# Matrix memory in a two-block kernel: gate rows spread over the partitions by DMA instead of by TensorE products

## Chip, cores and metric

One core of a Trainium2 chip. The metric is the device time of one execution, in microseconds (us).

## What is computed

Two transformer-like blocks over 512 tokens of width 1024, in float32. The first has sparse attention and a linear recurrence. The second has a matrix memory (mLSTM), a differential attention, a merge of the two and a mixture of 32 small experts. The change touches only the matrix memory, with 4 heads of 128 dimensions. Cut to what matters, the reference is:

```python
bcum = jnp.cumsum(ft, axis=-1)
dmat = jnp.where(causal, bcum[..., :, None] - bcum[..., None, :] + it[..., None, :], -jnp.inf)
m_t = jnp.maximum(m_inter, jnp.max(dmat, axis=-1))
s = jnp.einsum('bhtd,bhsd->bhts', qt, kt) * jnp.exp(dmat - m_t[..., None])
num = jnp.einsum('bhts,bhsd->bhtd', s, vt) + ...
den = jnp.maximum(jnp.abs(den), jnp.exp(-m_t))
h = num / den[..., None]
```

The kernel does not go by chunks of 64 with a carried state. It forms the whole causal 512 x 512 matrix of weights of a head, `exp(row[t] + column[s])` times the qk scores, in four strips of 128 keys.

## The kernel before

All engines run one long hand-ordered program. Every wait is written out, and a `Banks` object deals out the eight PSUM banks: `B.take(lo, hi, ...)` gives the banks from lo to hi - 1 in turn, and the wait on `u.free` is for the reader of that bank's last use. Each engine works through its functions in the order of `tensor_program`, `scalar_program`, `vector_program`, `pool_program` and `sync_program` (L3390 to L3544).

In block 2, projections write q, k, v and the gates. `dve_gates2` (L2079) computes the running sums of the gates with the heads in 4 partitions. Its results are `CI`, the column part, and `RA[j]` (4 partitions x 512), the row part for key strip j, valid from column 128 j. `CI` is turned into `COLI` (128 keys on the partitions). At the end of `pe_block2` (L1993) q and k of the differential attention are transposed into eight banks, which `act_block2` evicts (L2042).

Then comes the matrix memory: `pe_mlstm` (L2152), `act_mlstm` (L2180) and `dve_mlstm` (L2212), over heads h = 0 to 3 and key strips j = 0 to 3, with n = 512 - 128 j query columns. For each strip:

- PE: a row product (L2159) spreads row h of `RA[j]` over 128 partitions, into bank 0 or 1; it multiplies by a 4 x 128 selector made of one column of the identity.
- PE: the qk product (L2164), into bank 2, 3 or 4.
- DVE: adds the causal mask to the first 128 columns of the row, in PSUM (L2219).
- ACT: exponential with the column part as bias, PSUM to `WB[x]` in SBUF (L2192).
- DVE: multiplies qk scores, weights and a scale into `SB[h % 2]` (L2225).

After the strips PE computes a tile of the differential attention's values for the head (`vd`, `pe_tokens2`, L1938: eight chunks of 128 x 128 by 512 columns, two passes each), and then the last head's `mv` products (L2176), weights times values, with the row sum in column 129. ACT and DVE turn these into the normalised output (L2202 to L2236). The stage ends with the `mv` products of head 3. `pe_diff` (L2306) begins behind it.

On SP's queue, `sp_block2` (L1790 on) loads block 2's input weights in slots: `cm1` and `va` at L1800 and L1801, `om` at L1803, `vd` at L1805. `sp_merge2` (L2428) issues the two branch weights (`pm` L2431, `pd` L2432) when the last `va` product is done, then the gate weights in four parts (L2440, `part`), the late modulation weights and the output weight. `sp_experts` (L3103) starts with the merge's last output. `GBC` holds a row tile for the residual scaling later and is free during the matrix memory; `W[1]` holds the `va` weights until the last `va` product, and then `pd`.

Of the kernel before, what the change touches and what calls it, by code (L numbers as in the profile page):

```python
# [157 lines left out]
def build(nc, A, out, CD, COFF, CSMALL):  # L158
# [3 lines left out]
    def sig(*names, step=1):  # L162
        made = [Count(nc.alloc_semaphore(n), step) for n in names]
        counts.extend(made)
        return made if len(made) > 1 else made[0]
# [88 lines left out]
    xnd = nc.dram_tensor("scr_xn", [S, D], F32).ap()  # L254
    xd = nc.dram_tensor("scr_x", [S, D], F32).ap()
    modd = nc.dram_tensor("scr_mod", [2, D], F32).ap()

    o = 0

# [88 lines left out]
    CB = [omf[:, 0:1030], WIQ[:, 3072:4102]]  # L348
    HM, HD = QDR, KDR
    kdr = KDR.rearrange("p i d -> p (i d)")  # L350
    WB = [kdr[:, 1280:1792], PB2[0]]
    SB = [kdr[:, 0:1280], omf[:, 0:1280]]
    SB2 = [CV[0][:, 0:512], CV[1][:, 0:512]]
    HMT, HDT = QM, KM
# [66 lines left out]
    last_in = [sig(f"last_gates{e}_in", f"last_ups{e}_in", step=16) for e in (NP - 2, NP - 1)]  # L421
    exp_in = sig(*[f"expert{i}_in" for i in range(NE)], step=16)
    mod_out, mod_back = sig("mod_out", "mod_back", step=16)
    early_ada_in = sig("early_ada0_in", "early_ada1_in", step=16)
    part_in = sig("ada_half0_in", "ada_half1_in", step=16)
    b1_in = sig("b1_in", step=16)
# [1361 lines left out]
    def sp_block2(sp, ws):  # L1788
        ws.wait_ge(*B.use("pa", 7).full)
        sp.dma_start(WIQ.rearrange("p (c n) -> p c n", c=8), wsrc(w2in, 2048, 520)).then_inc(*ring[0].up("qd"))  # L1790
        ws.wait_ge(*B.use("wo", 2, 1).full)
        ws.wait_ge(*out7_pool.at("S", 4))
        sp.dma_start(wv(2, 8, 512), wsrc(w2in, 2568, 512)).then_inc(*ring[2].up("kd"))
        ws.wait_ge(*B.use("wo", 4, 1).full)
        sp.dma_start(wv(3, 8, 512), wsrc(w2in, 0, 512)).then_inc(*ring[3].up("cm0"))
        for i in range(NT - 1):
            sp_spill(sp, ws, i)
        sp_spill(sp, ws, NT - 1)
        ws.wait_ge(*B.use("kd", 4).full)
        sp.dma_start(wv(2, 8, 512), wsrc(w2in, 512, 512)).then_inc(*ring[2].up("cm1"))  # L1800
        sp.dma_start(wv(1, 8, 512), wsrc(w2in, 1024, 512)).then_inc(*ring[1].up("va"))  # L1801
        ws.wait_ge(*B.use("cm0", 4).full)
        sp.dma_start(wv(3, 8, 512), wsrc(w2in, 1536, 512)).then_inc(*ring[3].up("om"))  # L1803
        ws.wait_ge(*B.use("cm1", 4).full)
        sp.dma_start(wv(2, 8, 512), wsrc(w2in, 3080, 512)).then_inc(*ring[2].up("vd"))  # L1805

    def sp_spill(sp, ws, i):

# [343 lines left out]
    def pe_mlstm(pe, wp):  # L2152
        for h in range(5):
            if h < 4:
                for j in range(4):
                    n = 512 - 128 * j
                    u = B.take(0, 2, "row", h, j)
                    wp.wait_ge(*u.free)
                    pe.matmul(u.ap[:, 0:n], fv(ident[0:4, h:h + 1], [[0, 128]]), RA[j][0:4, 128 * j:512],  # L2159
                              start=True, stop=True).then_inc(*u.filled)  # L2160
                    u = B.take(2, 5, "mqk", h, j)
                    wp.wait_ge(*u.free)
                    wp.wait_ge(*qk_act.at(7))
                    pe.matmul(u.ap[:, 0:n], KM[:, h, tile(j)], QM[:, h, 128 * j:512], start=True, stop=True).then_inc(*u.filled)  # L2164
                pe_tokens2(pe, wp, "vd", 2, h, 7, 8)
            if h:
                for q in range(2):
                    u = B.take(5, 7, "mv", h - 1, q)
                    wp.wait_ge(*u.free)
                    wait_halves(wp, "va")  # L2170
                    wp.wait_ge(*set_dve.at("va"))
                    for i in (2 * q, 2 * q + 1):
                        for j in range(i + 1):
                            wp.wait_ge(*B.use("mqk", h - 1, j).out)
                            o0 = offs[j] + (i - j) * 128
                            t = pe.matmul(u.ap[:, 129 * (i % 2):129 * (i % 2) + 129], SB[(h - 1) % 2][:, o0:o0 + 128],  # L2176
                                          VA[:, j, h - 1, :], start=j == 0, stop=j == i)
                    t.then_inc(*u.filled)

    def act_mlstm(act, wa):  # L2180
        for h in range(5):
            if h < 4:
                for j in range(4):
                    n, x = 512 - 128 * j, (4 * h + j) % 2
                    u = B.use("row", h, j)
                    if h == 0 and j < 2:
                        wa.wait_ge(*B.use("dT", 1, 3).full)
                        wa.wait_ge(*B.use("ci").out)
                    else:
                        wa.wait_ge(*B.use("mqk", h - (j < 2), (j - 2) % 4).out)  # L2190
                    wa.wait_ge(*mw_dve.at("mask", h, j))
                    act.activation(WB[x][:, 0:n], u.ap[:, 0:n], ACT.Exp, bias=COLI[:, j, h:h + 1]).then_inc(*u.read)  # L2192
                u = B.use("vd", h)
                wa.wait_ge(*u.full)
                act.activation(VD[:, h, :], u.ap, ACT.Copy).then_inc(*u.read)
            if h:
                for q in range(2):
                    u = B.use("mv", h - 1, q)
                    if h > 1:
                        wa.wait_ge(*B.use("mv", h - 2, q).out)  # L2200
                    wa.wait_ge(*u.full)
                    act.activation(DEN[:, 2 * q:2 * q + 2], fv(u.ap[:, 128:129], [[129, 2]]), ACT.Abs).then_inc(*den_act.up(h - 1, q))  # L2202
                for i in range(NT):
                    wa.wait_ge(*B.use("mv", h - 1, i // 2).out)
                    if i > 1:
                        wa.wait_ge(*hm_act.at(h - 1, i - 2))
                    elif h > 1:
                        wa.wait_ge(*hm_act.at(h - 2, i + 2))
                    act.activation(kdr[:, 1792 + 128 * (i % 2):1920 + 128 * (i % 2)], HM[:, i, tile(h - 1)], ACT.Square,
                                   accum_out=HS3[:, 4 * i + h - 1:4 * i + h]).then_inc(*hm_act.up(h - 1, i))  # L2210

    def dve_mlstm(dve, wd):  # L2212
        for h in range(5):
            if h < 4:
                for j in range(4):
                    n, x = 512 - 128 * j, (4 * h + j) % 2
                    u = B.use("row", h, j)
                    wd.wait_ge(*u.full)
                    dve.tensor_tensor(u.ap[:, 0:128], u.ap[:, 0:128], k("masksT"), ALU.add).then_inc(*mw_dve.up("mask", h, j))  # L2219
                    v = B.use("mqk", h, j)  # L2220
                    if h > 1:
                        wd.wait_ge(*B.use("mv", h - 2, 1).full)
                    wd.wait_ge(*u.out)
                    wd.wait_ge(*v.full)
                    dve.scalar_tensor_tensor(out=SB[h % 2][:, offs[j]:offs[j] + n], in0=v.ap[:, 0:n], scalar=msc,  # L2225
                                             in1=WB[x][:, 0:n], op0=ALU.mult, op1=ALU.mult).then_inc(*v.read)
            if h:
                for q in range(2):
                    u = B.use("mv", h - 1, q)
                    d = DEN[:, 2 * q:2 * q + 2]  # L2230
                    wd.wait_ge(*den_act.at(h - 1, q))
                    dve.tensor_tensor(d, d, fv(COLM[:, 2 * q, h - 1:h], [[4, 2]]), ALU.max).then_inc(*den_dve.up("max", h - 1, q))
                    wd.wait_ge(*den_dve.at("max", h - 1, q))
                    dve.reciprocal(d, d).then_inc(*den_dve.up("r", h - 1, q))
                    wd.wait_ge(*den_dve.at("r", h - 1, q))
                    dve.tensor_tensor(HM[:, 2 * q:2 * q + 2, tile(h - 1)], fv(u.ap[:, 0:1], [[129, 2], [1, 128]]),  # L2236
                                      fv(d, [[1, 2], [0, 128]]), ALU.mult).then_inc(*u.read)
# [189 lines left out]

    def sp_merge2(sp, ws):  # L2428
        ws.wait_ge(*B.use("va", 4).full)
        ws.wait_ge(*qk_dve.at(7, 3))  # L2430
        sp.dma_start(wv(0, 4, 1024), wsrc(A["w_br_m_2"][0], 0, 1024)).then_inc(*ring[0].up("pm"))  # L2431
        sp.dma_start(wv(1, 4, 1024), wsrc(A["w_br_d_2"][0], 0, 1024)).then_inc(*ring[1].up("pd"))  # L2432
        for part in range(4):
            if part < 2:
                ws.wait_ge(*B.use(("vd", "om")[part], 3).full)
# [2 lines left out]
            w = W[2 + part % 2].rearrange("p (g c n) -> p g c n", g=2, c=8)  # L2438
            for n, g0 in enumerate((3592, 4616)):
                sp.dma_start(w[:, n], wsrc(w2in, g0 + 256 * part, 256)).then_inc(*ring[2 + part % 2].up("g2", part))  # L2440
            if part == 2:
                ws.wait_ge(*B.use("hmT", 3).full)
                ws.wait_ge(*B.use("hdT", 3).full)
# [1152 lines left out]
```

## Time and profile before

| | us |
|---|---|
| runs | 1286.52, 1273.55, 1278.89 |
| median of the three | 1278.89 |
| the profiled execution's own time | 1281.12 |
| span in its trace | 1279.3 |
| PE busy | 1204.9 (94%) |
| DVE busy | 593.0 (46%) |
| POOL busy | 312.6 (24%) |
| ACT busy | 307.8 (24%) |

Times in the trace count from the start of the span. PE stands for TensorE's products and PEld for its weight loads, which overlap them; DVE is VectorE, ACT ScalarE, POOL GpSimd, and SPq the queue in which SyncE issues transfers. The matrix memory's stage runs from about 651 to 718 us. A float32 product appears as two instructions (x2).

### The profile page before, as it was taken

How to read it: one execution, taken by the hardware profiler on the slowest of the kernel's cores; microseconds unless marked ns; L12 is line 12 of the kernel's file. 1: busy time of each engine (PE TensorE's matmuls, PEld its weight loads, DVE VectorE, ACT ScalarE, POOL GpSimd, SP SyncE). 2: the span in 40 equal slices, each digit the busy share in tenths (PEclk: the TensorE clock that was granted, in tenths of full speed). 3: DMA queues.
4: the chain of work that ended last, by engine and by line, in shares of the span. 5: the costliest groups of instructions: out<-in, count | busy, mean ns of one | idle time of the engine just before them, and what ended most of it. 6: DMA issues, size and time to landing. Idle time of an engine off the chain costs nothing.

```text
span 1279.3 us, 13740 instructions
## 1 busy us (share of the span) xinstructions
PE 1204.9 (94%) x5120; PEld 707.7 (55%) x5120; DVE 593.0 (46%) x1441; ACT 307.8 (24%) x715; POOL 312.6 (24%) x241
## 2 busy tenths in 40 slices
PE   7999999999999999999999999999899999988884
PEld 3555444445578444788855558577464674433342
DVE  2357375376632243259932476574442543222221
ACT  4302644343322001331122354100011321111110
POOL 7300012355571531264300300231100121211100
PEclk9999999999999999999989999999899999998998
DMA  9849105124224014105130202622449599999995
GB/s 317 183 149 273 66 1 132 66 91 140 70 96 169 28 67 142 56 6 192 67 131 1 67 1 66 203 90 75 99 176 350 195 333 389 409 399 406 413 401 203
DMA packets 95530, 214.97 MB, mean 168 GB/s; under 512 B 20190, under 2 KB 54382, under 8 KB 83640
## 3 DMA queue, kind: packets, MB, share of 16 engines
q1 hardware_dynamic: 81940, 192.62, 41.7%
q0 software_dynamic: 10320, 18.80, 6.0%
q10 hardware_dynamic: 3196, 2.61, 0.6%
q8 instruction: 43, 0.70, 0.2%
q14 instruction: 31, 0.25, 0.1%
HBM read 207.30 MB, written 14.75 MB: 174 GB/s over the span
## 4 chain that ended last, share of the span: by engine, by line
PE 70%; DVE 12%; SPq 8%; DMA 3%; ACT 3%; issue 2%; POOL 0%; POOLq 0%; DVEq 0%; ACTq 0%
PE PS L2533 8%; SPq L3084 7%; PE PS L1046 6%; PE PS L1496 4%; PE PS L1704 4%; PE PS L2712 4%; PE PS L2596 3%; PE PS L3216 3%; PE PS L673 3%; PE PS L1938 2%; PE PS L532 2%; DMA AN<-in_w_up 2%; PE PS L1950 2%; PE PS L1892 2%; PE PS L1524 2%; PE PS L1516 2%
## 5 line engine op out<-in xcount | busy, mean ns | idle before, releaser
L1046 PE MATMUL PS<-HT,W 128*128 128x512 f32 x256 | 125.4, 613 | 1.4 <-ACT AN L1210 1.4
L1310 POOL TENSOR_SCALAR AN<-AN,SM 128x128 f32<-128x128 f32 (+3 forms) x64 | 72.6, 1143 | 220.5 <-DVE SM L1418 220.5
L1344 DVE SCALAR_TENSOR_TENSOR AN<-AN,COLA 128x256 f32<-128x256 f32 x168 | 96.7, 576 | 6.1 <-DMA AN<-in_w_ada 1.0
L3216 PE MATMUL PS<-AN,HT 128*64 128x512 f32 x192 | 61.5, 632 | 9.8 <-DMA X<-in_w_up 6.0
L2511 POOL TENSOR_TENSOR AN<-W 128x512 f32<-128x512 f32 x8 | 10.2, 1271 | 235.3 <-DMA W<-in_w_in 99.7
L3301 DVE TENSOR_TENSOR HT<-HT,PS 128x256 f32<-128x256 f32 x16 | 6.7, 421 | 130.3 <-ACT HT L3276 130.3
L2596 PE MATMUL PS<-AN,W 128*128 128x512 f32 x128 | 58.7, 616 | 8.1 <-DVE AN L2652 8.1
L1046 PEld LDWEIGHTS PS<-HT,W 128*128 128x128 f32 x256 | 44.7, 194 | 39.0 <-issue 36.1
L2712 PE MATMUL PS<-W,AN 128*128 128x512 f32 x128 | 57.1, 595 | 0.0
L1291 ACT ACTIVATE AN<-PS,SM 128x128 f32<-128x128 f32 (+3 forms) x64 | 33.7, 526 | 94.7 <-DVE SM L1397 94.4
L3276 ACT ACTIVATE HT<-PS 128x256 f32<-128x256 f32 x16 | 6.1, 384 | 183.9 <-PE PS L3216 155.8
L3216 PEld LDWEIGHTS PS<-AN,HT 128*64 128x64 f32 x192 | 20.7, 145 | 47.8 <-issue 47.8
L2596 PEld LDWEIGHTS PS<-AN,W 128*128 128x128 f32 x128 | 25.0, 198 | 39.5 <-issue 28.8
L673 PE MATMUL PS<-W,HT 128*128 128x280 f32 (+1 forms) x128 | 43.6, 498 | 0.0
L3216 PE MATMUL PS<-W,HT 128*64 128x512 f32 x160 | 37.0, 616 | 5.7 <-DMA W<-in_w_up 5.7
L3237 PE MATMUL PS<-W,HT 128*64 128x512 f32 x160 | 36.5, 597 | 6.1 <-DVE HT L3306 6.1
L1385 DVE COPY AN<-PS 128x128 f32<-128x128 f32 (+3 forms) x32 | 15.6, 487 | 56.4 <-PE PS L1141 56.4
L2712 PEld LDWEIGHTS PS<-W,AN 128*128 128x128 f32 x128 | 23.5, 190 | 25.8 <-issue 25.8
L3158 POOL DMA_INDIRECT out<-GBC,SM x8 | 12.6, 1572 | 96.6 <-DVE GBC L3316 96.6
L3158 POOL DMA_INDIRECT out<-AN,SM x8 | 12.6, 1580 | 95.0 <-DVE AN L3316 69.1
L1141 PEld LDWEIGHTS PS<-K,AN 128*128 128x128 f32 x160 | 19.1, 142 | 26.6 <-issue 25.7
L673 PEld LDWEIGHTS PS<-W,HT 128*128 128x128 f32 x128 | 24.0, 190 | 17.5 <-issue 14.8
(566 smaller groups left out, 2474.2 us busy)
## 6 DMA issues: line engine op xcount, KB each, us to landing
W<-in_w_in SPq DMA_DIRECT2D x13, 2048.0 KB, 8.6
W<-in_w_down SPq DMA_DIRECT2D x20, 1024.0 KB, 27.6
AN<-in_w_gate SPq DMA_DIRECT2D x17, 1024.0 KB, 24.6
AN<-in_w_up SPq DMA_DIRECT2D x17, 1024.0 KB, 25.7
AN<-in_w_ada SPq DMA_DIRECT2D x16, 1024.0 KB, 6.0
AN<-in_w_down SPq DMA_DIRECT2D x12, 1024.0 KB, 26.6
W<-in_w_in SPq DMA_DIRECT2D x11, 1024.0 KB, 8.4
W<-in_w_gate SPq DMA_DIRECT2D x10, 1024.0 KB, 22.8
```

The costliest lines, as they stand in the source:

```text
L673: t = pe.matmul(u.ap[:, 0:nw], hT[:, c, tile(i)], wv(slot, 8, nw)[:, c, :], start=c == 0, stop=c == 7)
L1046: t = pe.matmul(u.ap, w[:, c, tile(m)], hT[:, c, :], start=c == 0, stop=c == 7)
L1310: pool.tensor_scalar(PU[u % 5][:, 0:n], PU[u % 5][:, 0:n], RSUM[:, u:u + 1], None, ALU.mult).then_inc(*sc_pool.up(u))
L1344: dve.scalar_tensor_tensor(out=a, in0=wt[:, c, :], scalar=ca["c2"][:, c:c + 1], in1=a, op0=ALU.mult, op1=ALU.add).then_inc(*ada_dve.up(p, c))
L1496: m = pe.matmul(u.ap[:, 256 * h:256 * h + 256], s[:, c, tile(2 * pair + h)], t[:, c, :], start=c == 0, stop=c == 3)
L1704: m = pe.matmul(u.ap, t[:, c, tile(j)], s[:, c, :], start=c == 0, stop=c == 3)
L2533: m = pe.matmul(u.ap[:, 0:256], s[:, c, :], t[:, c, :], start=c == 0, stop=c == 3)
L2596: t = pe.matmul(u.ap, wv(n, 4, 1024)[:, c, tile(m)], (HMT, HDT)[n][:, c, :], start=c == 0, stop=c == 3)
L2712: t = pe.matmul(u.ap, MT2[:, c, i, :], wv(2 + n, 8, 512)[:, c, :], start=c == 0, stop=c == 7)
L3084: sp.dma_start(WE[m % NE][:, 2048 * n:2048 * n + 2048], src).then_inc(*exp_in[m % NE].up(m))
L3216: t = pe.matmul(u.ap[r, :].rearrange("p (n f) -> p n f", n=2), XGT[e % 2][:, c, r], w_gu(3 * e + half)[:, c], start=c == 0, stop=c == 7)
L3237: t = pe.matmul(u.ap[r, :], AT[e % 2][:, c, r], w_dn(m, half)[:, c, n * 512:(n + 1) * 512], start=c == 0, stop=c == 1)
```

## The change

The row products leave TensorE. `RA[0]` to `RA[3]` are written to a scratch tensor `rowd` [4, 1280] in DRAM, the valid columns of the four strips side by side (offsets `offs` = 0, 512, 896, 1152). For each head one transfer then reads row h of it with a partition step of 0 and fills a [128, 1280] tile `WB[h]` in SBUF: head 0 in `GBC`, heads 1 to 3 in `W[1]`. The mask is added and the exponential taken in place there. The four masks of a head now stand together (`dve_row_masks`), those of head h+1 behind the score products of head h. The qk products get the banks 0 to 4. Transfers: the four writes and row 0's load go into `sp_block2` ahead of the load of `om`, with a wait for the writes; the loads of rows 1 to 3 go ahead of `pm`; `pd`, whose slot they use, moves behind the gate weights' part 0 and a wait for the last score product.

```diff
+    rowd = nc.dram_tensor("scr_row", [4, 1280], F32).ap()
-    WB = [kdr[:, 1280:1792], PB2[0]]
+    WB = [GBC[:, 0:1280]] + [W[1][:, 1280 * n:1280 * n + 1280] for n in range(3)]
...
         sp.dma_start(wv(1, 8, 512), wsrc(w2in, 1024, 512)).then_inc(*ring[1].up("va"))
+        ws.wait_ge(*if_dve.at("ra", 3))
+        for j in range(4):
+            n = 512 - 128 * j
+            sp.dma_start(rowd[:, offs[j]:offs[j] + n], RA[j][0:4, 128 * j:512]).then_inc(*gate_row_out.up())
+        ws.wait_ge(*sg_act.at("ga", 0))
+        ws.wait_ge(*gate_row_out.at())
+        sp_row(sp, ws, 0)
         ws.wait_ge(*B.use("cm0", 4).full)
...
+    def sp_row(sp, ws, h):
+        row = rowd[h:h + 1, :]
+        sp.dma_start(WB[h], bass.AP(tensor=row.tensor, offset=row.offset, ap=[[0, 128], [1, 1280]])).then_inc(*gate_row_in[h].up())
... pe_mlstm
-                    u = B.take(0, 2, "row", h, j)
-                    wp.wait_ge(*u.free)
-                    pe.matmul(u.ap[:, 0:n], fv(ident[0:4, h:h + 1], [[0, 128]]), RA[j][0:4, 128 * j:512],
-                              start=True, stop=True).then_inc(*u.filled)
-                    u = B.take(2, 5, "mqk", h, j)
+                    u = B.take(0, 5, "mqk", h, j)
... act_mlstm
-                    act.activation(WB[x][:, 0:n], u.ap[:, 0:n], ACT.Exp, bias=COLI[:, j, h:h + 1]).then_inc(*u.read)
+                    act.activation(v, v, ACT.Exp, bias=COLI[:, j, h:h + 1]).then_inc(*mw_act.up(h, j))
... dve_mlstm
+    def dve_row_masks(dve, wd, h):
+        wd.wait_ge(*gate_row_in[h].at())
+        for j in range(4):
+            d = WB[h][:, offs[j]:offs[j] + 128]
+            dve.tensor_tensor(d, d, k("masksT"), ALU.add).then_inc(*mw_dve.up("mask", h, j))
...
+        dve_row_masks(dve, wd, 0)
+        wd.wait_ge(*B.use("dT", 1, 3).full)
...
-                    dve.tensor_tensor(u.ap[:, 0:128], u.ap[:, 0:128], k("masksT"), ALU.add).then_inc(*mw_dve.up("mask", h, j))
...
+                if h < 3:
+                    dve_row_masks(dve, wd, h + 1)
... sp_merge2
         ws.wait_ge(*B.use("va", 4).full)
+        for h in range(1, 4):
+            sp_row(sp, ws, h)
         ws.wait_ge(*qk_dve.at(7, 3))
-        sp.dma_start(wv(1, 4, 1024), wsrc(A["w_br_d_2"][0], 0, 1024)).then_inc(*ring[1].up("pd"))
...
+            if part == 0:
+                ws.wait_ge(*B.use("mqk", 3, 3).out)
+                sp.dma_start(wv(1, 4, 1024), wsrc(A["w_br_d_2"][0], 0, 1024)).then_inc(*ring[1].up("pd"))
```

## Rows read from the trace of the kernel before

**Rows 1.** The page: each engine's busy time, its share of the span, instructions.

```profile
PE 1204.9 (94%) x5120; PEld 707.7 (55%) x5120; DVE 593.0 (46%) x1441; ACT 307.8 (24%) x715; POOL 312.6 (24%) x241
```

**Rows 2.** Busy time by stretch, us (x instructions), then PEclk, DMA share, GB/s.

```profile
core 0: us, PE busy (x) PEld busy (x) DVE busy (x) ACT busy (x) POOL busy (x), PEclk, DMA share, GB/s
...
691.20:705.50 14.30, 14.30 (x51) 7.08 (x49) 4.09 (x14) 3.90 (x15) 0.00 (x0) 1.00 0.00 0
...
720.00:775.00 55.00, 52.98 (x213) 27.36 (x212) 41.14 (x155) 27.94 (x99) 10.13 (x8) 1.00 0.03 7
```

**Rows 3.** The chain that ended last, in order of time: start, length, what.

```profile
706.31 6.87 PE PS L1938 x16
713.18 2.25 PE PS L2176 x20
716.53 1.84 PE PS L2176 x14
...
781.68 20.74 PE PS L2533 x96
...
1120.43 1.88 SPq L3084
```

**Rows 4.** Timeline, heads 0 and 2: start, length, engine, instruction, [idle before].

```profile
651.15 1.12 PE L2159 MATMUL PS<-AN,K 4*128 4x512 f32 x2 [0.57 <-ACT AN L2042]
...
659.36 9.45 PE L1938 MATMUL PS<-W,HT 128*128 128x512 f32 x16
...
685.40 1.12 PE L2159 MATMUL PS<-AN,K 4*128 4x512 f32 x2
...
686.45 1.13 PE L2164 MATMUL PS<-AN 128*128 128x512 f32 x2
...
687.50 0.91 PE L2159 MATMUL PS<-AN,K 4*128 4x384 f32 x2
...
688.34 0.91 PE L2164 MATMUL PS<-AN 128*128 128x384 f32 x2
...
691.17 7.03 PE L1938 MATMUL PS<-W,HT 128*128 128x512 f32 x16
```

**Rows 5.** Timeline, ACT: the eight evictions ahead of the stage.

```profile
647.57 4.03 ACT L2042 ACTIVATE AN<-PS 128x512 f32<-128x512 f32 x8 [4.94 <-PE PS L1993]
```

**Rows 6.** PE alone by stretch: busy us (x), PEclk, DMA share, GB/s.

```profile
651.15:653.00 1.85, 1.85 (x4) 1.00 1.03 423
653.00:659.36 6.36, 6.36 (x14) 0.58 0.88 355
659.36:664.10 4.74, 4.74 (x7) 0.50 0.00 0
...
668.73:674.56 5.83, 5.83 (x18) 0.99 0.00 0
674.56:677.60 3.04, 3.04 (x5) 0.50 0.02 5
677.60:683.07 5.47, 5.47 (x13) 0.98 0.00 0
```

**Rows 7.** Groups of 646 to 722 us by form: busy us, mean ns | idle before.

```profile
L2219 DVE TENSOR_TENSOR PS<-PS,K 128x128 f32<-128x128 f32 x16 | 4.7, 294 | 15.5 <-PE PS L2159 15.4
...
L2192 ACT ACTIVATE AN<-PS,SM 128x512 f32<-128x512 f32 x4 | 2.7, 677 | 0.9 <-DVE PS L2219 0.8
...
L2192 ACT ACT_TABLE_LOAD x1 | 1.3, 1283 | 1.1 <-DVE PS L2219 1.1
```

**Rows 8.** Timelines of DVE and of SP's queue ahead of the stage.

```profile
572.48 0.27 DVE L2095 TENSOR_TENSOR AN<-AN 4x128 f32<-4x128 f32 x1
...
573.87 0.58 SPq L1801 DMA_DIRECT2D W<-in_w_in  x1
597.62 0.37 SPq L1803 DMA_DIRECT2D W<-in_w_in  x1
...
646.39 0.37 SPq L2431 DMA_DIRECT2D W<-in_w_br_m  x1
```

**Rows 9.** DMA issues of the whole run: queue, x, KB each, median us to landing.

```profile
AN<-scr_line POOLq DMA_DIRECT2D x1, 1024.0 KB, 17.2
...
scr_line<-AN POOLq DMA_DIRECT2D x1, 64.0 KB, 5.1
```

More of the change, by code:

```diff
@@ L423, in build @@
     mod_out, mod_back = sig("mod_out", "mod_back", step=16)
+    gate_row_out = sig("gate_rows_out", step=16)
+    gate_row_in = sig(*[f"gate_row{h}_in" for h in range(4)], step=16)
     early_ada_in = sig("early_ada0_in", "early_ada1_in", step=16)
@@ L2183, in act_mlstm @@
                 for j in range(4):
[L2184 to L2187, printed above, removed]
+                    v = WB[h][:, offs[j]:offs[j] + 512 - 128 * j]
+                    if h == 0 and j == 0:
                         wa.wait_ge(*B.use("ci").out)
-                    else:
-                        wa.wait_ge(*B.use("mqk", h - (j < 2), (j - 2) % 4).out)
                     wa.wait_ge(*mw_dve.at("mask", h, j))
-                    act.activation(WB[x][:, 0:n], u.ap[:, 0:n], ACT.Exp, bias=COLI[:, j, h:h + 1]).then_inc(*u.read)
+                    act.activation(v, v, ACT.Exp, bias=COLI[:, j, h:h + 1]).then_inc(*mw_act.up(h, j))
                 u = B.use("vd", h)
@@ L2215, in dve_mlstm @@
                 for j in range(4):
-                    n, x = 512 - 128 * j, (4 * h + j) % 2
-                    u = B.use("row", h, j)
-                    wd.wait_ge(*u.full)
-                    dve.tensor_tensor(u.ap[:, 0:128], u.ap[:, 0:128], k("masksT"), ALU.add).then_inc(*mw_dve.up("mask", h, j))
+                    n = 512 - 128 * j
                     v = B.use("mqk", h, j)
@@ L2222, in dve_mlstm @@
                         wd.wait_ge(*B.use("mv", h - 2, 1).full)
-                    wd.wait_ge(*u.out)
+                    wd.wait_ge(*mw_act.at(h, j))
                     wd.wait_ge(*v.full)
                     dve.scalar_tensor_tensor(out=SB[h % 2][:, offs[j]:offs[j] + n], in0=v.ap[:, 0:n], scalar=msc,
-                                             in1=WB[x][:, 0:n], op0=ALU.mult, op1=ALU.mult).then_inc(*v.read)
+                                             in1=WB[h][:, offs[j]:offs[j] + n], op0=ALU.mult, op1=ALU.mult).then_inc(*v.read)
+                if h < 3:
+                    dve_row_masks(dve, wd, h + 1)
             if h:
```

## The prediction

> **What bounds the kernel now.** I read the page first. TensorE (PE) is busy for 94% of the span [rows 1], so the question is whether the stream around the change is PE's own. The table by stretch comes next: from 691.2 to 705.5 us, one head of the matrix memory, PE is busy all the time while DVE and ACT are busy for 4.1 and 3.9 of 14.3 us [rows 2]. The chain of waits says the same. It runs through the value products of line 1938 and the products of line 2176, head after head, up to 716.53 + 1.84 = 718.4 us. After that it goes on through the differential attention, the merge and the routing, in pieces of PE, DVE and ACT, and enters SP's queue of expert loads at 1120 us, where transfers hold it [rows 3]. None of the pieces from 718 to 1120 us is a transfer or tied to a fixed time; each begins when the stage before has given it something, and the first expert load waits for the merge. So what the memory's stage gives up should move the rest of the program as a block.
>
> Inside a head PE's order is: four times a row product and a qk product, then 16 value products (eight chunks, two passes each). The row products stand in that stream in full view. In head 2, where nothing waits and the clock is full, the block from 685.40 to the first value product at 691.17 is 5.77 us long. Its starts split it: 1.05 us for a row product of 512 columns, 0.84 for 384, so 0.21 for each 128, which gives 0.63 and 0.42 for the other two. Row products take 2.94 us, and 2.83 are left for the qk products [rows 4]. In head 0 the same block takes 659.36 - 651.15 = 8.21 us: a later row product waits for its bank, and for that DVE's mask, ACT's exponential and DVE's product have to run.
>
> **The change part by part.**
>
> *Row products removed.* Heads 1, 2 and 3 are each shorter by about 2.9 us at full clock (head 1's block is 5.83 us long [rows 6], head 3's like head 2's): 8.8 us.
>
> *Head 0.* The qk products now take the banks 0 to 4 in turn, so in head 0 they wait for no DVE or ACT work of this stage. The first needs bank 0, which the old first row product got at 651.15. Bank 1 is free when the last transpose is evicted, at 647.57 + 4.03 = 651.60 [rows 5], before the second product wants it at 652.20. The block takes 2.83 us in place of 8.21: 5.4 us gained.
>
> *The clock.* The granted clock was 1.00 up to 653, 0.58 on average to 659.36, 0.50 to 664.10 and again from 674.56 to 677.60 [rows 6]; in the later heads it was 1.00 [rows 2]. Both falls come in or just behind a block of row and qk products, the first with waits in it, and both times the value products that follow, one behind the other, brought the clock back to its full level of 2.4 GHz. Head 0's value products took 668.73 - 659.36 = 9.37 us and head 1's 683.07 - 674.56 = 8.51 [rows 6], against 6.87 in head 3 [rows 3]. Without the thin stretches I expect both at 6.87: 2.5 + 1.6 = 4.1 us gained. This is the least certain term, because PE never stopped for more than 0.57 us before the first fall [rows 4].
>
> The Trainium skill ("TensorE: Matmul & The Clock Gate", Part 1) says that the array's clock falls after it has been idle. By that sentence alone row products that keep PE busy are not to blame, the low clock stays, and the 4.1 us drop out of the sum. The same page's section on a second failure mode reports falls from many short stops between groups, which keeps them in. No row here decides between the two.
>
> *Mask and exponential.* The 16 mask additions took 0.29 us each in PSUM, an exponential at most 0.68 us, its table load 1.28 [rows 7]. They stay, with operands in SBUF. A 128-column addition in SBUF took 0.27 us on DVE [rows 8]; bounds for the 16 are half and twice that, 2 to 9 us, in a stage in which DVE is free for over two thirds. The masks of head h+1 stand behind the products of head h; the exponentials of head 0 start at 651.60 + 1.28 = 652.9 and end by 655.6. PE comes back to bank 0 with head 1's second product at about 662. Nothing is added to the sum. If this cover were gone, one head's chain (1.28 + 2.7 + 0.7 us) would be the price, once.
>
> *Row writes and row 0, in SP's queue.* The rows are ready at 572.48 + 0.27. Four writes from 4 partitions follow the loads of line 1801 (573.87), then SP waits for them and issues row 0's spread load, all before the load of `om` at 597.62 [rows 8]. Two 2 MB loads are ahead in the queue. The nearest row for the writes is 64 KB to DRAM from 8 partitions, landed after 5.1 us [rows 9]; bounds are 5 us and, behind 4.2 MB at 423 GB/s [rows 6], 15 us. The spread load is 128 partitions x 5 KB = 0.66 MB, all from the same 5 KB; the trace has no such load of that size. The nearest is the bias line's read, 1 MB into 128 partitions from overlapping addresses, landed after 17.2 us beside other transfers, 61 GB/s [rows 9]. The other end is the rate of the weights at 651 us, 423 GB/s. So row 0 is in between about 583 and 600 us, and it is needed at 651. `om`, needed at 718, may leave some 5 us late. Cost zero.
>
> *Rows 1 to 3* leave at 646.39, ahead of the two branch weights [rows 8]. At 61 GB/s they land at 657, 668 and 679, at 423 GB/s before 656 even with five microseconds for the landing. In the new stream head 1's exponentials follow head 0's value copy at about 661, head 2's come at 673, head 3's at 685. I take the slow end: slack 4 to 6 us. The first branch weight is in by 685 and needed behind the gate products that end at 802 [rows 3]. Cost zero.
>
> *The second branch weight* moves behind the first gate weights, to about 695 us. DMA is nearly idle there (0.03 from 720 to 775 us [rows 2]) and its product comes after 802. Cost zero.
>
> *Sum.* 5.4 + 2.5 for head 0, 2.9 + 1.6 for head 1, 2.9 + 2.9 for heads 2 and 3: 18.2 us. The stage built anew says the same: 651.15 + 2.83 + 6.87 = 660.9; head 1 at 670.6, head 0's values 2.3 us to 672.9, head 2 at 682.6, values to 684.9, head 3 at 694.6, and 5.4 us of last values as now: 700.0 against 718.4. The profiled run took 1281.12 us, so 1262.9. The median of the runs shown, 1278.89, is 2.2 us lower, which puts the changed kernel at 1260.7; I say 1261.
>
> **The rivals.**
>
> *The clock stays low* (0.20). If the fall at 653.9 has its cause before the stage, it stays in place: 10.2 us at 0.50 under a dense stream cost 5.1, and the second fall's 3.0 us cost 1.5. The gain is then 13.1 without the second fall, 11.6 with it: 1266 to 1267 us. For it: PE had been thin for under 3 us when the clock fell. Against: the blocks of heads 2 and 3, which wait for nothing, are followed by full clock. By the idle rule of the Trainium skill named above it would come out so.
>
> *The gain is given back later* (0.12). The differential stage starts on ACT's chain, the experts end on bandwidth. If the merge or the expert loads keep their present time, all but a few microseconds are lost, some 1277 us. Against: the chain shows no transfer and no fixed time between the stage and the experts [rows 3].
>
> *A spread load that is too slow* (0.06), the other side. 128 reads of the same 5 KB might crawl. They hold up the stage when row 1 lands after 660, row 2 after 673 or row 3 after 685, that is under 1.97 MB / 38.6 us = 51 GB/s. The whole gain is gone when row 3 lands at 703 (35 GB/s); at 28 GB/s it lands at 716 and the kernel ends at 1279 + 13 = 1292. Against it stand the 61 GB/s of the bias line.
>
> **How the numbers follow.** The forecast has 0.62: 1261 us. The three runs shown lie 13 us apart, so a median may miss the sum by 5 us; its own range is 1255 (the lowest run less 18.2) to 1266. To leave no more than 2 in 10 outside, the range reaches through the clock case, seen from the highest run: 1286.5 - 14 = 1272. I give 1254 to 1272. What a measurement can tell from no change is about 1%, 12.8 us. Of the forecast 0.57 lie beyond it, of the clock case half, 0.10, and 0.02 of the late losses, which may be partial: faster 0.69. Slower is the slow load but for 0.01: 0.05. The rest, 0.26, is the same.
>
> **What would show it.** Right: head 0's block of qk products 2.8 to 3.0 us long; the value products of all heads 6.9 us, with the granted clock at 1.00 from 651 on; the first differential product 49 us after the first product of head 0, where it was 67; rows 1 to 3 landed within 33 us; merge and experts as long as now. Wrong: 0.50 early in the stage (first rival); DVE idle on a DMA before the masks (third); a later stage longer by what this one gave up (second).

## The result and the profile after

| us | before | after |
|---|---|---|
| median | 1279.13 (4 runs, 1273.55 to 1286.52) | 1259.83 (4 runs, 1258.83 to 1263.15) |
| profiled execution | 1281.12 | 1263.15 |
| its span | 1279.3 | 1261.3 |
| first product of head 0 to first differential product | 67.13 | 45.94 |

The ratio is 0.9841, with an interval of 0.9805 to 0.9877: 1.6% faster, clear of no change. Six further runs of the changed kernel gave 1259.62 and 0.9849 (0.9814 to 0.9884). The prediction was 1261.0 us, and the stage was to end 49 us after its start.

The page's first part (busy us, share of the span, instructions) stands against [rows 1]: PE has 32 instructions and 18.7 us of work less (and PEld 32 weight loads), and DVE, ACT and POOL have what they had.

```profile
PE 1186.2 (94%) x5088; PEld 702.6 (56%) x5088; DVE 592.2 (47%) x1441; ACT 306.7 (24%) x715; POOL 312.4 (25%) x241
```

The timeline of PE in the changed kernel (start, length, instruction, idle before) answers to [rows 4]. Line 2175 is now the qk product, 1953 the value product, 2187 `mv`, 2330 the first product of the differential attention.

```profile
651.63 2.42 PE L2175 MATMUL PS<-AN 128*128 128x512 f32 x8 [0.57 <-ACT AN L2057]
653.89 7.03 PE L1953 MATMUL PS<-W,HT 128*128 128x512 f32 x16
660.76 2.32 PE L2175 MATMUL PS<-AN 128*128 128x512 f32 x8
662.91 7.03 PE L1953 MATMUL PS<-W,HT 128*128 128x512 f32 x16
...
697.57 0.49 PE L2330 MATMUL PS<-AN 64*128 64x128 f32 x4
```

Head 0's qk block is 653.89 - 651.63 = 2.26 us long, head 1's 2.15, and the value products of both take 6.9. PE by stretch (length, busy us, granted clock, DMA share, GB/s), against [rows 6], has the clock at 1.00 in every stretch; the first and one of the later ones:

```profile
651.60:660.90 9.30, 9.27 (x25) 1.00 0.79 316
...
681.20:692.40 11.20, 11.20 (x46) 1.00 0.00 0
```

What the change put on SP's queue and its time from issue to landing (queue, x, KB each, median us), against [rows 8, 9]:

```profile
574.99 4.29 SPq L1808 DMA_DIRECT2D scr_row<-AN  x4
587.82 0.35 SPq L1820 DMA_DIRECT2D GBC<-scr_row  x1
...
646.87 1.29 SPq L1820 DMA_DIRECT2D W<-scr_row  x3
```

```profile
W<-scr_row SPq DMA_DIRECT2D x3, 640.0 KB, 5.6
...
GBC<-scr_row SPq DMA_DIRECT2D x1, 640.0 KB, 4.0
```

The four writes, issued from 574.99 us behind two loads of 2 MB, are done when row 0's load leaves at 587.82. Row 0 is in SBUF at 592 us, 60 us before it is needed. Rows 1 to 3 leave at 646.9 and are in by about 655. The masks and the exponentials by form (x | busy us, mean ns | idle before) wait for no transfer; they cost about what they cost in PSUM [rows 7]:

```profile
L2223 DVE TENSOR_TENSOR W<-W,K 128x128 f32<-128x128 f32 x12 | 2.7, 282 | 0.0
...
L2199 ACT ACTIVATE W<-W,SM 128x512 f32<-128x512 f32 x3 | 2.1, 708 | 0.0
```

**Where the gain went.** The stage is 21.2 us shorter, the span 18.0. The distance between the same instruction in the two traces tells where 3.2 us went. The stage starts 0.48 us later in the profile after (651.63 against 651.15), less than the same kernel's start moves from run to run (see the experiments). The first differential product stands 20.7 us earlier, the first gate product (line 2533 before, 2551 after) 774.38 - 754.84 = 19.5, and so does the whole merge up to the routing. There the chain of waits of before and of after (start, length, what) parts again:

```profile
1026.91 3.58 PE PS L2758 x20
...
1033.30 2.43 PE PS L2758 x20
```

```profile
1007.26 4.43 PE PS L2776 x20
...
1015.21 2.43 PE PS L2776 x20
```

1026.91 - 1007.26 = 19.65, 1033.30 - 1015.21 = 18.09. Between the two the clock is at 0.50 in both kernels, but it comes back later in the changed one. PE by stretch, before and after:

```profile
1025.00:1029.00 4.00, 3.48 (x17) 0.50 1.02 423
1029.00:1033.00 4.00, 4.00 (x43) 0.95 0.86 288
```

```profile
1006.00:1010.00 4.00, 3.48 (x17) 0.50 1.01 407
1010.00:1015.00 5.00, 5.00 (x44) 0.69 0.75 260
```

From there on the distance stays at 18.1 us as long as PE sets the pace. Where the expert loads do, behind 1120 us of the kernel before, the distance between the same loads swings between 15 and 20 us (1200.24 - 1180.52 = 19.7, 1231.03 - 1214.81 = 16.2), and it is back at 18.0 in the end. So the end moved with the rest, but the loads between do not keep one distance. Why the clock came back later in the routing is not shown. The loss of 1.2 us in the differential stage is the subject of the fourth experiment.

### The profile page after: what moved, and what is told of

It reads as the page before. It is cut to its first block, busy times and chain, and to the rows that moved or that the text cites. A ratio compares the mean times of both kernels' runs of the same rounds, so it can differ in the third digit from the quotient of the medians.

```text
span 1261.3 us, 13671 instructions
## 1 busy us (share of the span) xinstructions
PE 1186.2 (94%) x5088; PEld 702.6 (56%) x5088; DVE 592.2 (47%) x1441; ACT 306.7 (24%) x715; POOL 312.4 (25%) x241
## 4 chain that ended last, share of the span: by engine, by line
PE 68%; DVE 13%; SPq 9%; DMA 3%; ACT 3%; issue 2%; POOL 0%; POOLq 0%; DVEq 0%; ACTq 0%
PE PS L2551 8%; SPq L3102 7%; PE PS L1049 6%; PE PS L1499 4%; PE PS L1707 4%; PE PS L2730 4%; PE PS L2614 4%; PE PS L676 3%; PE PS L3234 3%; PE PS L535 2%; DMA AN<-in_w_down 2%; PE PS L1965 2%; PE PS L1907 2%; PE PS L1527 2%; PE PS L1953 2%; PE PS L1519 2%
```

## The experiments

A single execution says little of the total here: the start of the stage lay between 646 and 654 us in the kernels below, behind the same code, and at 651.63 and 646.24 us in two profiles of the changed kernel itself. So they are compared by the length of the stage (first product of head 0 to first differential product), which the changed kernel repeats to 0.1 us: 45.94 in its first profile, 692.18 - 646.24 = 45.94 in another.

### 1. The row products put back, DMA path kept

```diff
@@ pe_mlstm, after the waits for the bank
+                    pe.matmul(u.ap[:, 0:n], fv(ident[0:4, h:h + 1], [[0, 128]]), RA[j][0:4, 128 * j:512],
+                              start=True, stop=True)
                     pe.matmul(u.ap[:, 0:n], ...
```

Nobody reads these products; the qk product overwrites them in the same bank.

> The changed kernel with the 16 row products put back into TensorE's stream, each ahead of its qk product and into the same bank, which the qk product then overwrites; nobody waits for them and the rows still come by DMA. Stage length is from the first product of head 0 to the first differential product: 67.1 us before the change, 45.9 after. Stream theory: each head's block grows from 2.16 us back to the 5.77 us of head 2 before, 4 x 3.6 = 14.4 us, stage 60.3 us, granted clock 1.00 throughout; the remaining 6.8 us to 67.1 are head 0's waits (2.4) and the low clock (4.1). Rival, thin products alone lower the clock: 0.50 early in the stage also here, head 0's value products above 9 us, stage 64 us or more. Rival, pure product time: 1280 columns at four passes and 2.4 GHz are 2.1 us per head, stage 54.4.

Measured: 1279.20 us (one run; before 1279.01, median of 7), the stage 718.77 - 651.65 = 67.12 us, to 0.01 that of before. The first rival came true, thin products alone lower the clock; the stream theory had 60.3. Its PE timeline, and PE by stretch:

```profile
651.65 1.12 PE L2175 MATMUL PS<-AN,K 4*128 4x512 f32 x2 [0.57 <-ACT AN L2057]
652.70 1.13 PE L2177 MATMUL PS<-AN 128*128 128x512 f32 x2
...
654.86 1.65 PE L2177 MATMUL PS<-AN 128*128 128x384 f32 x2
...
660.05 9.24 PE L1953 MATMUL PS<-W,HT 128*128 128x512 f32 x16
```

```profile
655.00:657.00 2.00, 2.00 (x3) 0.50 1.01 414
657.00:660.05 3.05, 3.05 (x8) 0.50 0.62 254
...
675.00:678.00 3.00, 3.00 (x6) 0.50 0.02 5
```

So in this stage the transfers, the masks in SBUF and the new place of the exponentials cost nothing together, and its whole gain is that of the products. (Behind it this kernel has the change's loss too: 775.95 - 718.77 = 57.18 us from the first differential product to the first gate product, where the kernel before has 56.10.) Head 0's block is 660.05 - 651.65 = 8.40 us long, though no product in it waits for a reader. The clock falls before 655 and again just before 675, as it did in the kernel before [rows 6], while PE is busy without a gap. In the kernel before the waits of head 0 were there, but behind the half clock they cost nothing more.

### 2. Row products over 4, 32, 64 and 128 partitions

```diff
@@ the same place; K = 128, 64 or 32
+                    pe.matmul(u.ap[:, 0:n], fv(ident[0:K, h:h + 1], [[0, 128]]), QM[0:K, h, 128 * j:512],
+                              start=True, stop=True)
```

Again nobody reads these products. With 32 and more partitions they take the q rows (`QM`), since `RA` has only 4.

> As the run with the row products put back, but each of them has 128 partitions in place of 4 (an identity column against the q rows, the result overwritten). If the 0.2 us and more that each row and each qk product took beyond its columns come from changing between 4 and 128 partitions, the block is 2 x 2.16 = 4.3 us and the stage 45.9 + 8.6 = 54.5 us. If they come from anything else in two products in turn, the stage is 60.3 us as with 4 partitions.

> Row products put back as in the first run, without a reader, with 64 partitions in place of 4 (4: stage 67.1 us, blocks of 5.8 us, clock down twice; 128: 54.6 us, blocks of 4.3 us, clock 1.00). Theory one: each change of the number of partitions costs 0.2 us whatever the numbers are, so the block is 5.8 us again, and the clock depends on how much of the array is fed, so that it stays at 1.00 with half of it: stage 60.3 us. Theory two: change and clock go together and depend on the small number of 4: block 4.3 us, stage 54.6. Theory three: as with 4, 67.1 us.

> The same with 32 partitions. Theory one (a cost per change, a clock that follows what is fed): block 5.8 us and the clock down at least once, stage 62 to 67 us. Theory two (only 4 is too few): 54.6 us.

| partitions | block, us | stage, us | clock | total, us |
|---|---|---|---|---|
| none (the change) | 2.16 | 45.94 | 1.00 | 1259.83 (4 runs) |
| 128 | 4.3 | 700.97 - 646.39 = 54.58 | 1.00 | 1261.94 (one run) |
| 64 | 5.78 | 709.14 - 648.53 = 60.61 | 1.00 | 1270.03 (one run) |
| 32 | 5.78 | 710.20 - 649.60 = 60.60 | 1.00 | 1273.65 (one run) |
| 4 | 5.77 where the clock is full | 67.12 | two falls | 1279.20 (one run) |

The stage with 128 partitions was forecast at 54.5 us, and theory one held with 64. With 32 both theories missed: the change has its price, and the clock stays up.

The chain of the kernel with 128 partitions has each product at 0.86 us for 512 columns, row or qk, and 0.65 for 384:

```profile
657.84 0.86 PE PS L2175 x2
658.70 0.86 PE PS L2177 x2
659.56 0.65 PE PS L2175 x2
```

That of the kernel with 32 partitions has 1.05 and 0.84, 0.2 us more for each, whatever its columns. PE by stretch shows the clock full and PE without a gap:

```profile
650.72 1.06 PE PS L2177 x2
651.77 0.84 PE PS L2175 x2
652.61 0.84 PE PS L2177 x2
```

```profile
649.60:655.50 5.90, 5.90 (x17) 1.00 1.01 408
```

Two things follow. Going from a product over fewer partitions to one over all 128, or back, costs 0.2 us; a head has eight such changes, and (60.60 - 54.58) / 32 = 0.19 us. It is the same for 4, 32 and 64 partitions. And in this stage the clock fell only with 4. The decomposition of the 21.2 us is then one of measured differences: 54.58 - 45.94 = 8.6 for the products' columns, 6.0 for the changes, 67.12 - 60.60 = 6.5 for the clock.

The Trainium skill ("TensorEngine Tiling (Array Packing)", Key Properties) says that changing the tiling mode drains TensorE, with no price. The 0.2 us per change agree with it in kind. That TensorE drains is not seen in the trace, which books the 0.2 us as busy time.

### 3. Row products in groups of four

```diff
@@ pe_mlstm: four row products, then the four qk products
-                for j in range(4):
+                us = [B.take(0, 5, "mqk", h, j) for j in range(4)]
+                for j, u in enumerate(us):
...
+                    pe.matmul(u.ap[:, 0:n], fv(ident[0:4, h:h + 1], [[0, 128]]), RA[j][0:4, 128 * j:512],
+                              start=True, stop=True)
+                for j, u in enumerate(us):
```

> As the run with the row products put back (4 partitions), but the four row products of a head stand together ahead of its four qk products, so that TensorE changes between 4 and 128 partitions twice per head and not eight times. Change theory: the block is 2.16 + 2.16 + 2 changes of about 0.2 = 4.7 us, stage 45.9 + 4 x 2.5 = 56 us. If the order does not matter, 60.3 us.

Measured: 1275.59 us (one run), the stage 709.41 - 650.12 = 59.29 us, where 56 had been forecast for a full clock. Two changes in place of eight leave a block of 2.35 + 2.35 = 4.70 us where the clock is full (5.77 before), as the price of 0.2 us asks. The 3.3 us above that forecast are the clock's: it still fell behind the row products of heads 0 and 2, whose qk products took 3.52 and 3.27 us in place of 2.35, and their value products 7.39 and 7.63. So alternating is not what makes the clock fall.

### 4. The second branch weight moved behind part 1

The changed kernel loses 1.2 us between the first differential product and the first gate product (57.27 us in place of 56.10). In the timelines POOL, whose eight additions prepare part 0 of the gate weights, starts 702.30 - 697.57 = 4.73 us behind the first differential product, before 3.31 us. Before:

```profile
721.59 1.27 POOL L2511 TENSOR_TENSOR AN<-W 128x512 f32<-128x512 f32 x1 [99.66 <-DMA W<-in_w_in]
...
732.32 0.35 DVE L2381 SCALAR_TENSOR_TENSOR AN<-AN,SM 128x128 f32<-128x128 f32 x1
```

After:

```profile
702.30 1.26 POOL L2529 TENSOR_TENSOR AN<-W 128x512 f32<-128x512 f32 x1 [79.88 <-DMA W<-in_w_in]
...
711.67 1.44 DVE L2395 SCALAR_TENSOR_TENSOR AN<-AN,SM 128x128 f32<-128x128 f32 x1
```

DVE's product of two tiles in SBUF takes 1.44 us beside POOL's additions and 0.35 when they have ended. POOL's eight take 10.7 us from 721.59 and from 702.30, to 732.3 and 713.0; that third product falls behind their end before, and inside after. The Trainium skill ("SBUF — State Buffer", "Who interferes with whom") says that a VectorE instruction with two SBUF inputs contends with a GpSimd one that reads SBUF, for a pair of ports that is locked by one of them: 1.44 against 0.35 us beside operations of 1.27 us agrees.

Why did POOL start later? The load of `pd` was issued right behind part 0's (693.55, the one after 692.49). The experiment puts it behind part 1's:

```diff
-            if part == 0:
+            if part == 1:
                 ws.wait_ge(*B.use("mqk", 3, 3).out)
                 sp.dma_start(wv(1, 4, 1024), wsrc(A["w_br_d_2"][0], 0, 1024)).then_inc(*ring[1].up("pd"))
```

> The changed kernel with the load of the second branch weight moved from behind the gate weights' part 0 to behind part 1. Theory: beside it part 0 landed 1.4 us later against the differential stage, GpSimd's eight additions began 4.7 us instead of 3.3 us behind the first differential product and lay over one more of DVE's 1.44 us products (0.35 us without GpSimd beside it). Here GpSimd starts at 3.3 us, and the stretch from the first differential product to the first gate product falls from 57.3 to 56.1 us; the time falls by 1.2 us. Rival: the 1.2 us have another cause, and both stay. Risk: the second branch weight is now issued some 60 us later, still 30 us ahead of its product.

Measured: 1259.11 us (4 runs, 1257.21 to 1264.19), a ratio of 0.9850 (0.9811 to 0.9888) to before, no different from the change itself. POOL starts 697.53 - 692.85 = 4.68 us behind the first differential product, as late as ever, and from there to the first gate product it is 57.2 us. POOL by stretch, with the DMA share and GB/s last, and POOL's first addition:

```profile
694.80:695.80 1.00, 0.00 (x0) 1.00 0.57 171
695.80:696.80 1.00, 0.00 (x0) 1.00 0.05 7
```

```profile
697.53 1.26 POOL L2529 TENSOR_TENSOR AN<-W 128x512 f32<-128x512 f32 x1 [79.84 <-DMA W<-in_w_in]
```

The theory falls, and its rival holds: alone on the DMA engines, part 0 has moved nearly all its bytes 7.6 us after its issue at 687.78, as before (713.21 to 720.8), and yet POOL starts 2 us after that and not 0.8. In every kernel with the new transfers it started 9.3 to 10 us behind the issue, in the two without them (before and the sixth below) 8.4.

What holds POOL is one late piece of the load. Part 0's two loads are spread over the 16 DMA engines, and the trace records 32 landings. In the kernel before, the last comes 8.3 us after the issue and POOL starts 0.1 us behind it. In this experiment 31 have come by 8.3 us and one comes at 9.6, and POOL starts 0.1 us behind that one. The share of 0.05 in the second stretch above is what is left of it, 0.8 of one engine. The loads' median time to landing, over 30 us from part 0's issue on, before:

```profile
W<-in_w_in SPq DMA_DIRECT2D x2, 1024.0 KB, 6.6
```

In this experiment, with a queue (packets, MB, share) that has no packet in that stretch of the kernel before:

```profile
q8 instruction: 1, 0.02, 0.2%
...
W<-in_w_in SPq DMA_DIRECT2D x2, 1024.0 KB, 7.3
```

That one packet, 16 KB of instructions, starts 7.2 us behind part 0's issue and takes 1.16 us; the last ten packets of the load start behind its end, from 8.35 us on. In all eleven traces of kernels with the new transfers such a packet starts between 1.1 and 7.3 us behind the issue, and one landing comes 0.9 to 1.6 us behind the other 31. In the two traces without them it starts 0.9 us ahead of the issue, and none is late. So a fetch of instructions on one of the engines that carry the load is what the traces point to. They do not name the engine of a packet, no run moved the fetch on purpose, and why it falls there in the eleven is not shown. What the late start costs is 1.44 - 0.35 = 1.09 us on the third product, most of the 1.2 us above.

### 5. The square root moved out of the differential stage's head

```diff
@@ act_om
-        if step == 0:
-            wa.wait_ge(*hm_act.at(3, 3))
-            act.activation(HR3[:, 0:16], HS3[:, 0:16], ACT.Sqrt, bias=eps, scale=1.0 / 128).then_inc(*om_act.up("root"))
@@ act_om_gate, and DVE's reciprocal of it in dve_om
+        wa.wait_ge(*hm_act.at(3, 3))
+        act.activation(HR3[:, 0:16], HS3[:, 0:16], ACT.Sqrt, bias=eps, scale=1.0 / 128).then_inc(*om_act.up("root"))
```

With the stage before it shorter, the differential attention still starts on ACT's chain: a square root with its table load, 1.28 + 0.31, and a second table load of 1.28 stand ahead of the first exponential.

> The changed kernel with the square root of the matrix memory's norms moved from the first step of the differential attention to its end, ahead of the sigmoid (and DVE's reciprocal of it ahead of the gating). In the changed kernel's trace ACT loads a table for the root at 699.45 and one back for the exponential at 701.07, and DVE waits for the root. Theory, the chain of waits runs through this and everything behind moves with it: the first exponential of the stage comes 2.9 us earlier (5.5 us behind the first differential product now, 2.6 then), and the time falls by 2 to 2.9 us. Rival, the stage gives it back because PE or DVE bound it anyway, or the table load that is now at the end of the stage is on the path there: within 1 us of the changed kernel.

Measured: 1259.74 us (4 runs, 1255.35 to 1262.73), 0.9849 (0.9791 to 0.9907), the time of the change and not 2 us less. The same kernel again, beside the unaltered change on one chip:

> The changed kernel again, unaltered, as the partner of the next run on the same chip: 1255 to 1263 us, a ratio to the kernel before of 0.982 to 0.989. The stage from the first product of head 0 to the first differential product is 45.9 us again.

> The changed kernel with the square root of the matrix memory's norms, and DVE's reciprocal behind it, at the end of the differential stage in place of its first step. Theory: the 3.0 us by which the first exponential comes earlier, 1.3 us of which were left at the first gate product, stay to the end: 1 to 2 us below its unaltered partner in the median, a ratio to it of 0.998 to 0.999. Rival: the runs of one kernel lie 5 us apart, and the clock's falls behind the stage take it back, so the medians lie within 1 us or the other way round.

Measured: 1259.62 (6 runs) for the change, 1263.13 (6 runs, 1258.75 to 1266.19; 0.9871, 0.9834 to 0.9909) with the root moved. ACT's timeline shows that the edit does what it should: the first exponential starts 1.8 us behind the first differential product at 695.77, where it was 702.36 - 697.57 = 4.8.

```profile
697.54 0.35 ACT L2374 ACTIVATE AN<-PS,SM 128x128 f32<-128x128 f32 x1
```

The gate products start 56.0 us behind it in both profiles, 1.3 earlier than in the change. PE by stretch shows what took part of the 3.0 us back, in the first profile and in the second:

```profile
714.00:718.00 4.00, 4.00 (x9) 0.57 0.00 0
```

```profile
714.00:722.00 8.00, 7.18 (x21) 0.79 0.00 1
```

The clock falls there, which it does not in the change. PE had been idle for 0.82 us some 2 us before the first of these falls, and no 4-partition product is near; what brings them is not shown. The total gives no gain, and the theory of 1 to 2 us misses: the two sets of runs differ by 3.4 us for the same kernel, more than the edit could bring, and the intervals overlap. It is no version to prefer.

### 6. The alternative without DMA: row products padded to 128 partitions

On the kernel before. `RA` is set to zero on all 128 partitions, and the product uses a whole column of the identity; the extra terms are zeros.

```diff
@@ kernel before
+        for j in range(4):
+            dve.memset(RA[j][:, 0:512], 0.0).then_inc(*set_dve.up("ra0", j))
+        wd.wait_ge(*set_dve.at("ra0", 3))
         dve_gates2(dve, wd)
...
-                    pe.matmul(u.ap[:, 0:n], fv(ident[0:4, h:h + 1], [[0, 128]]), RA[j][0:4, 128 * j:512],
+                    pe.matmul(u.ap[:, 0:n], fv(ident[:, h:h + 1], [[0, 128]]), RA[j][:, 128 * j:512],
```

> The kernel before, with row products, masks and exponentials as they were, but the four row tiles are cleared to zero on all 128 partitions ahead of the gates and the row products take 128 partitions (the full column of the identity as selector). No transfer of rows. If the cost of the row products was half their columns and half their 4 partitions, the blocks fall from 5.77 to 4.3 us and the clock stays at 1.00: stage 67.1 to 54.6 us, 12.5 us less, some 1266.5 us, against 1260 for the change. Rival: with the stream denser the chain of mask, exponential and product holds the banks, head 0's block stays at 6 us or more and the gain is 8 us or less.

Measured: 1269.56 us (10 runs, 1265.02 to 1273.44), a ratio of 0.9930 (0.9905 to 0.9955). The stage is 710.70 - 653.91 = 56.79 us long, 10.3 shorter than before, with the products still there. That lies between the forecast (12.5 shorter) and its rival (8 or less). PE's timeline and its first stretch:

```profile
657.48 0.70 PE L2162 MATMUL PS<-AN,K 128*128 128x256 f32 x2 [0.30 <-ACT AN L2195]
...
659.02 0.49 PE L2162 MATMUL PS<-AN,K 128*128 128x128 f32 x2 [0.41 <-ACT AN L2195]
```

```profile
653.90:659.70 5.80, 5.08 (x17) 1.00 1.03 418
```

Now head 0's waits for a bank are seen, 0.7 us of them as idle time, and its block is 659.57 - 653.91 = 5.66 us long against 4.4 with 128 partitions and no reader (experiment 2); the clock is full in spite of them. So of the two suspects for the fall of the clock, thin 4-partition products and short stops, it is the products: with the same stops and 128 partitions the clock stays, without stops and with 4 partitions (the first experiment) it falls. The rows are the same in both, padded with zeros here, so it is not their values either. Between 4 and 32 partitions the operand changed too, so there the number of partitions is not the only difference.

### 7. Differential qk products over all partitions

The output is not the reference's: each product of line 2330 sums over both halves of the head's dimensions.

```diff
-                    pe.matmul(u.ap[:, 0:n], QDT[pr, h, tile(i)], KDT[pr, h, 0:n], start=True, stop=True)...
+                    pe.matmul(u.ap[:, 0:n], QDT[:, h, tile(i)], KDT[:, h, 0:n], start=True, stop=True)...
```

> The changed kernel, with the 32 strips of the differential attention's qk products (line 2330) taken over all 128 partitions in place of the 64 of one half, so each product holds the sum over both halves and the output differs. The number of columns, and with it PE's work by columns, stays the same. Theory: what PE loses when it goes from products of one number of partitions to products of another (about 0.2 us each in the runs with 4, 32 and 64 partitions beside 128) is lost in this stage too, wherever PE sets the pace; the first 16 steps from the first differential product to the first gate product, 57.3 us in the changed kernel, come out 2 to 5 us shorter, and a single pair of products at full clock 0.2 us shorter. Rival: the stage goes at the pace of DVE and ACT, so it stays within 0.5 us of 57.3 and PE shows more idle time instead. All other stages unchanged; total 1255 to 1262 us.

Measured: 1266.50 us (one run), and from the first differential product to the first gate product 759.89 - 699.85 = 60.04 us, 2.8 longer than in the change. Both expectations missed. PE's timeline in one late step, the change first:

```profile
742.57 1.13 PE L2330 MATMUL PS<-AN 64*128 64x512 f32 x4
743.63 1.98 PE L2264 MATMUL PS<-W,HT 128*128 128x512 f32 x4
745.45 0.49 PE L2340 MATMUL PS<-K,AN 128*128 128x128 f32 x3
```

```profile
746.15 1.88 PE L2330 MATMUL PS<-AN 128*128 128x512 f32 x4
747.87 1.88 PE L2264 MATMUL PS<-W,HT 128*128 128x512 f32 x4
749.58 0.49 PE L2340 MATMUL PS<-K,AN 128*128 128x128 f32 x3
```

Two products of 512 columns over all partitions take 1.72 us (746.15 to 747.87). Two over 64, one in each half of the partitions, take 1.06 (742.57 to 743.63): the columns of one, 0.86, and the 0.2 of one change. The pair runs side by side. A step is 3.97 us long in the change (742.57 to 746.54) and 4.43 here (746.15 to 750.58): 0.86 us for the second product's columns, less 0.40 for two changes. For the strips of 128 columns, where the columns weigh 0.21, the full products win by 0.17 (period 2.16 against 2.33 us). So the price of 0.2 us for a change holds in this stage too, and what was overlooked is what the halves give. The Trainium skill ("TensorE: Matmul & The Clock Gate", Part 3) says that products in different row groups of the array run concurrently; the trace agrees.

## Why the prediction came out right

**Its mechanism was right.** PE's own stream set the stage's time, the row products stood in it in full view, and what the stage gave up moved the program behind it. Of the signs that it listed, the value products of 6.9 us, the clock at 1.00 from 651 on and the rows landed within 33 us are there. The qk block was to be 2.8 to 3.0 us long and is 2.15 to 2.26; the stage was to be 49 us long and is 45.9; merge and experts were to take as long as now, and the way to them grew by 1.2 us in the differential stage and 1.6 in the routing.

**The size of the row products was off.** The block of 5.77 us was split into 2.94 for the rows and 2.83 for the qk products, from starts that seemed to give 0.21 us for each 128 columns and the same 0.2 on top for every product [rows 4]. The 0.2 was taken for a part of a product. It is the price of the change to the other number of partitions, so it leaves the qk products as well: heads 2 and 3 gave 5.77 - 2.15 = 3.6 us each, not 2.9. A row of the same trace could have told: the value products, 16 instructions of 512 columns, take 6.87 us [rows 3], that is 0.86 for two, and two instructions of the qk product beside the rows took 1.05. That is 0.7 us a head, 2.7 in all.

**The waits of head 0 (2.4 us of its 5.4) and the clock (4.1) were one term.** The prediction had the long block wait for banks. Experiment 1 has a block of 8.40 us without a wait, so all 6.5 us were the clock's, and experiment 2 measured them as 6.5. [rows 6] could have told: from 653.00 to 659.36 PE was busy for all 6.36 us, at a clock of 0.58. The sum was right for a split that was not. The rival that the clock stays low had the right price, 5.1 + 1.5 = 6.6 us for the two falls.

**The clock.** The 4.1 us were called the least certain term, with 0.20 on the rival that they stay. In this stage the fall came with the 4-partition products, without any stop (experiments 1 and 3), and it did not come with 32, 64 or 128 partitions without stops (experiment 2), nor with 128 and two stops of 0.30 and 0.41 us (experiment 6). The stop of 0.57 us ahead of the stage is in all these kernels. By the idle rule of the Trainium skill ("TensorE: Matmul & The Clock Gate", Part 1) the low clock would have stayed; this case's runs speak against it as the cause here, and against the short stops of the same page's second failure mode as well. Elsewhere the clock is low without such products (the routing, and the differential stage of experiment 5), so they are not its only cause. Why 4 partitions and not 32 remains open.

**The terms at zero held.** Spread loads were bounded by 61 and 423 GB/s; 640 KB took 4.0 us with little beside it, some 160 GB/s with the landing in it, and 5.6 us in the median of three. Experiment 1 confirms the zero for the whole DMA path and the SBUF operands in this stage, whose length is that of before. The masks kept 0.28 us.

**The give-back was a matter of size.** Its rival had all but a few microseconds lost at the expert loads. Of 21.2 us, 0.5 lie in the start, 1.2 in the differential stage, 1.6 in the routing's half clock. The second of these was not in the prediction: a load that lands late on one DMA engine starts POOL later, and one more DVE product meets POOL. The third is not explained. So the sum of 18.2 met a span 18.0 us shorter, and medians 19.3 apart, because terms that were too small by 3.0 us were met by 3.2 us that came to be lost. That the two are so near is chance.

## What to carry to other kernels

Look at the partitions (K) in PE's rows, not only at the columns. In this kernel a product over few partitions cost its columns in full and 0.2 us more at each change from and to full ones, and with 4 partitions it pulled the clock to half for the products behind it too. Spreading a row by products is cheaper over 128 partitions padded with zeros (10.3 us of this stage's 21.2), and a load with a partition step of 0, issued early, removes it altogether. When a trace shows a regular surplus of 0.2 us in a product, compare it with the same shape elsewhere in the trace before it is booked as its cost. When an engine waits for a load whose bytes seem to have arrived, look at the landings: one DMA engine may still be busy.

## What had not been expected of the hardware

- The change between products over 128 partitions and products over 4, 32 or 64 costs 0.2 us on PE, the same for all three, and shows as busy time.
- The granted clock fell to 0.50 with PE busy without a gap, when 4-partition products stood in the stream, alternating or in groups of four; with 32, 64 and 128 in the same place it stayed at 1.00.
- Two products over the lower and the upper 64 partitions took 1.06 us for 512 columns each, a change included, where two over 128 took 1.72.
- One of the 32 landings of a 2 x 1 MB load came 0.9 to 1.6 us behind the others in all eleven traces in which a 16 KB packet of instructions started while the load was under way, and none was late in the two in which it had started before the load's issue. The engine that waited started with the last landing.
- A load of 128 x 5 KB, all from one row of 5 KB in DRAM, landed 4.0 us after its issue, faster than the 17.2 us of the 1 MB of overlapping reads that it was bounded by [rows 9].
